# One GpSimd subtraction of 1024 columns in place of four of 256, in a float32 block whose weights are split in two

## The reference

```python
u = rmsnorm(x, norm_mix) * (1 + scale1) + shift1        # scale, shift, gate from cond @ ada_w
aq, ak, av, bq, bkv, biq, bik, biw, cq, ck, cv, g = split_cols(u @ w_in)
y_a, y_b, y_c = diff_attention(...), dsa_attention(...), moba_attention(...)   # each @ its own w_br
x = x + gate1 * ((gates[0]*y_a + gates[1]*y_b + gates[2]*y_c) @ w_o)
x = x + gate2 * (square(relu(u2 @ w_ff1)) @ w_ff2)
for layer in range(2):                                  # the second block
    proj = rms_norm(x, pre_norm[layer]) @ w_in_2[layer]
    y_conv = c_b * causal_depthwise_conv(c_c * c_x) * silu(c_z)
    y_ret = retention_chunkwise(rotary(q), rotary(k), v), normalised, * silu(r_z)
    x = x + rms_norm(concat(y_conv, y_ret) @ w_out[layer], post_norm[layer])
```

## Time and profile before

| | us |
|---|---|
| median of three runs | 1036.79 |
| the three runs | 1036.6, 1036.79, 1037.68 |
| the profiled execution, its own time | 1037.68 |
| its span in the profile | 1035.6 |
| busy: PE, DVE, ACT, POOL | 971.7, 597.0, 489.9, 737.7 |

### The profile page before, as it was taken

One profiled execution on the slowest core, in us unless ns is written; L12 is line 12 of the kernel. 1 busy time (PEld: TensorE's weight loads), 2 busy tenths in 40 slices (PEclk: granted clock), 3 DMA queues, 4 the chain that ended last, 5 costly groups with the idle time before them and its releaser, 6 DMA issues.

```text
span 1035.6 us, 21952 instructions
## 1 busy us (share of the span) xinstructions
PE 971.7 (94%) x7796; PEld 946.8 (91%) x7796; DVE 597.0 (58%) x978; ACT 489.9 (47%) x803; POOL 737.7 (71%) x916
## 2 busy tenths in 40 slices
PE   0599999999899999999999999999999999999997
PEld 0598889899789999999999999999999999999996
DVE  5748896664888555111465557765245555676612
ACT  2344656554345555444344446444444444644441
POOL 6666746666785888777466667999746666699973
PEclk9999999999999999999899999999999999999999
DMA  8956445555553546645244444554523444454521
GB/s 324 382 199 244 164 163 203 204 187 185 198 204 122 204 162 216 240 174 181 103 164 163 151 146 153 205 197 164 180 107 122 163 162 155 138 196 166 199 103 41
DMA packets 28079, 184.68 MB, mean 178 GB/s; under 512 B 3011, under 2 KB 5488, under 8 KB 6128
## 3 DMA queue, kind: packets, MB, share of 16 engines
q1 hardware_dynamic: 25832, 167.54, 45.0%
q10 hardware_dynamic: 2184, 16.27, 4.3%
HBM read 182.73 MB, written 1.07 MB: 177 GB/s over the span
## 4 chain that ended last, share of the span: by engine, by line
PE 83%; DVE 10%; ACT 3%; issue 2%; POOL 1%; DMA 1%; SPq 0%; POOLq 0%; DVEq 0%; ACTq 0%
PE mm L518 24%; PE mm L520 24%; PE mm L519 23%; DVE ada_acc L1342 3%; PE mm L551 1%; PE mm L539 1%; PE mm L540 1%; PE mm L541 1%; PE ps_t L578 1%; DVE w_lo L1320 1%; DMA ada_raw<-ada 1%; ACT w_hi L941 1%; PE ps_s L839 1%; PE ps_o L854 1%; PE ps_o L890 1%
## 5 line engine op out<-in xcount | busy, mean ns | idle before, releaser
L423 POOL TENSOR_TENSOR w_lo<-raw,w_hi 128x256 fp32r<-128x256 f32 x872 | 699.1, 836 | 244.2 <-ACT w_hi L941 243.5
L518 PE MATMUL mm<-u_hi,w_hi 128*128 128x256 f32 x1608 | 466.3, 290 | 1.9 <-issue 1.9
L520 PE MATMUL mm<-u_hi,w_lo 128*128 128x256 f32 x1608 | 454.8, 283 | 0.0
L519 PE MATMUL mm<-u_lo,w_hi 128*128 128x256 f32 x1608 | 454.8, 283 | 0.0
L941 ACT ACTIVATE w_hi<-raw 128x1024 fp32r<-128x1024 f32 x291 | 306.8, 1055 | 167.2 <-PE mm L520 167.2
L518 PEld LDWEIGHTS mm<-u_hi,w_hi 128*128 128x128 f32 x1608 | 308.1, 192 | 8.0 <-issue 7.5
L519 PEld LDWEIGHTS mm<-u_lo,w_hi 128*128 128x128 f32 x1608 | 308.2, 192 | 2.1 <-issue 1.9
L520 PEld LDWEIGHTS mm<-u_hi,w_lo 128*128 128x128 f32 x1608 | 307.9, 191 | 0.0
L1320 DVE TENSOR_TENSOR w_lo<-raw,w_hi 128x1024 fp32r<-128x1024 f32 x72 | 94.1, 1307 | 122.6 <-ACT w_hi L941 120.8
L518 PE MATMUL mm<-mix_hi,w_hi 128*128 128x256 f32 x256 | 71.9, 281 | 0.2
L520 PE MATMUL mm<-h_hi,w_lo 128*128 128x256 f32 x256 | 71.9, 281 | 0.0
(11 more groups left out here) (280 smaller groups left out, 1305.7 us busy)
## 6 DMA issues: line engine op xcount, KB each, us to landing
raw<-weights SPq DMA_DIRECT2D x145, 1024.0 KB, 4.8
ada_raw<-ada ACTq DMA_DIRECT2D x14, 1024.0 KB, 4.9
ada_raw<-ada SPq DMA_DIRECT2D x6, 1024.0 KB, 8.0
ada_more<-ada SPq DMA_DIRECT2D x4, 1024.0 KB, 9.2
bias<-tab_scratch SPq DMA_DIRECT2D x1, 1536.0 KB, 10.6
dec<-decay ACTq DMA_DIRECT2D x1, 1536.0 KB, 7.1
x<-xT SPq DMA_DIRECT2D x1, 1024.0 KB, 15.3
out<-x SPq DMA_DIRECT2D x4, 256.0 KB, 2.2
```

Of the source, the lines that this page charges most:

```text
L423: ins = nc.gpsimd.tensor_tensor(w_lo[:, s, at], r[:, at], hi[:, at], ALU.subtract)
L518: nc.tensor.matmul(dst, wh, rhs_hi(k), start=a, stop=False)
L519: nc.tensor.matmul(dst, wh, rhs_lo(k), start=False, stop=False)
L520: i = nc.tensor.matmul(dst, wl, rhs_hi(k), start=False, stop=b)
```

## The change

In POOL's `low`, the four subtractions over a quarter of the unit each (256 columns) become one over all 1024 columns. The semaphore `lo_pool` was raised by the last of the four and is now raised by the one instruction, by the same amounts. Nothing else changes: the same units, the same waits ahead of them, the same slots.

```diff
             r = raw[:, (c // 2) % RAW_PAIRS, (c % 2) * KC * P:(c % 2 + 1) * KC * P]
             s = c % SLOTS
-            hi = w_hi[:, s, :].bitcast(F32)
-            quarter = KC * P // 4
-            for e in range(4):
-                at = slice(e * quarter, (e + 1) * quarter)
-                ins = nc.gpsimd.tensor_tensor(w_lo[:, s, at], r[:, at], hi[:, at], ALU.subtract)
-            ins.then_inc(S["lo_pool"], 3 if c == 2 else 2 if c % 4 == 2 else 1)
+            nc.gpsimd.tensor_tensor(w_lo[:, s, :], r, w_hi[:, s, :].bitcast(F32), ALU.subtract)\
+                .then_inc(S["lo_pool"], 3 if c == 2 else 2 if c % 4 == 2 else 1)
```

## The result

The changed kernel takes 1107.95 us in the median of four runs (1103.44 to 1108.39), the one before 1037.24 in the same comparison (1036.6 to 1039.5, four runs). The ratio is 1.065, with a 95% interval of 1.062 to 1.068: slower by 71 us. The prediction had the direction, and a size of 24.6 us. It is wrong by a factor of almost three. In all, 39 executions of the changed kernel are on record, in two groups: 21 between 1100.3 and 1104.3 us and 18 between 1106.6 and 1110.8. By its span the profiled one belongs to the lower group.

A forecast was written before the change was run, and what follows sets the result against it. The prediction took PE as the bound (busy 94%, 83% of the chain), with DVE on 10% of the chain. Gains of 3.3 and losses summed to +24.6 on 1036.8 us: 1061.4, say 1061, range 1041 to 1080.

The forecast's parts named there:

- Price of the long operation: POOL's subtraction over 1024 columns: 2.33 us, against 2.90 for four pieces; bounds 2.0 and 2.9.
- Rival 1: The lock is let go within the long instruction, so only gains stay: 1032 us; chance 0.07.
- (a) to (c): Start-up and one later unit: PE gets w_lo sooner, gains of 1.3, 1.6 and 0.4, together -3.3 us.
- (d): Retention heads: POOL holds kr, PE waits; six turns at 1.36 and two at 0.8 make +9.8 us.
- kr(0): The earlier kr in a retention turn: no longer slips in between two pieces, POOL is first, +0.33 us.
- kr(1): The later kr in a retention turn: held by POOL, +0.5 us alone; both kr's late together, 1.36 a turn.
- (e): End of the convolution heads, twice: three POOL units delay DVE's tail, PE waits 3.4 each, +6.8 us; the loop costs nothing.
- (f): Branch outputs, 258 to 284: six POOL units each cost DVE 1.73, 10.4 less 5.1 lost today: +5.3 us.
- (g): Output projection and norm, 288.75 to 313: six units at 1.7, less 4.2 lost today and 3 idle: +3.0 us.
- (h): Attention, 103 to 139: five contacts at 1.7, less 4 today, a third covered by waits for ScalarE: +3 us.
- Feed-forward and out-projections: FFN (323 to 498) and two later output projections: PE sets the pace, 0, bounds -0.5 to +2 us each.
- Rival 3: DVE's lags pile up in four convolution and feed-forward loops, 2 to 5 us each: 1078 us; chance 0.12.

The follow-up runs named there:

- E3: The changed kernel with four pieces again for the units of the retention heads (135 to 166, 215 to 246): 1089.39 us, ratio 1.049.
- E7: The changed kernel with ScalarE's copy mix_hi of the retention output one unit later in its order: 1101.28 us, ratio 1.061.
- E12: The kernel before, with one long instruction for units 55 to 70 (branch outputs, output projection and norm): 1049.16 us, ratio 1.011.
- E11: The kernel before, with one long instruction for units 25 to 54 (attention from 139 us on): 1048.34 us, ratio 1.012.
- E9: POOL does every unit in eight pieces of 128 columns, against four in the kernel before: 1084.88 us, ratio 1.047.
- E6: The kernel before, with one long instruction for the last eight units of each convolution stage: 1052.49 us, ratio 1.017.

## Why the prediction was right in kind and wrong in size

- **Price of the long operation:** 2.33 predicted, 2.34 at least and 2.41 in the median. Right.
- **The lock holds for a whole instruction at 1024 columns:** right, by kr at 573.89. Rival 1 is out. DVE's growth of 131 us was put at 30 to 90.
- **(a) to (c), start-up and w_lo:** -2.9 and -0.4 predicted, -3.6 and -0.8 (unit 74) measured. Right.
- **(d) Retention heads:** +9.8 predicted, 1.36 a turn; +11.8 measured, 1.45 a turn, and E3 returns 12.3. Right in size, with both kr's late in each turn. Its two parts were split otherwise: kr(0) costs 0.69 and not 0.33 (the rows of the prediction make that 0.29), kr(1) another 0.76 and not 1.03.
- **(e) Convolution heads: this is the step that failed.** It said that DVE "lags by some 2 us per turn of four units and holds there", and costed the loop at nothing, on the cover of PE's four banks. DVE's lag doesn't hold. Three blocked operations of 5.7 us in all make its turn 12.98 us long, against PE's 11.52, so the lag grows from turn to turn. Nor is it the banks that PE meets first, but w_lo, POOL's behind ScalarE's late w_hi and DVE's own; only with ScalarE's copy moved (E7) is it the banks. The loops cost 4.9 and 5.2. The end was put at 3.4 with DVE arriving on time; it arrives late, and PE's wait of 6.8 is followed by 6 us at half clock, a cost for which the prediction had no term. 6.8 predicted, 28 measured. The prediction named the price of being wrong, "2 us more for each layer" without cover, but as a cost per layer and not as one that piles up.
- **(f) Branch outputs:** +5.3 predicted, +6.7 measured (E12: +6.3). Right in size. It isn't m_lo, as I had said, but the sum of two SBUF tiles, merged, that is hit six times in eight units at 2.05 to 2.52 us; m_lo is now at 418 ns throughout (the earlier trace rows had 942).
- **(g) Output projection and norm:** +3.0 predicted, +7.8 measured (E12: +6.8). The mechanism is the one named; too small by the average of 1.7 per contact less "4.2 lost today", where three contacts in a row end on PE's wait for acc, and by the clock of 0.80.
- **(h) Attention:** +3 predicted for 103 to 139, and +3.1 measured for units 7 to 18, all of it at unit 16 (115 us before the change). But the stage goes on to 246. From 139 on I had no term at all, because the chain that I read ended there, and units 19 to 50 lose 12.1 (E11: 10.8). PE waits there for DVE's prob (4.0 us, 0 before), for ScalarE's o_var (4.3, before 1.1) and a little longer for two others; which contacts make these late was not taken apart.
- **Feed-forward and out-projections:** 0 predicted. No loss (-1.8 with its norms).

By size the missing 40 us (64.4 - 24.6) are: 21 in (e), 12 in the part of attention without a term, 5 in (g), 3.4 in (d) and (f), less 2.1 of greater gains where w_lo comes sooner and at the norms. Rival 3, lags that pile up, comes nearest. It had 0.12 and, at 1078, was itself too low. Of its four loops the two of the convolution heads lose 4.9 and 5.2, the top of its 2 to 5, by the in-order queue of ScalarE that it named; the feed-forward loops lose nothing. The 12 us in attention were in no rival.

The changed kernel's median, 1107.95, is of its upper group, some 6 us above the profiled execution; no trace shows where those are.

## What to carry to other kernels

In this kernel a VectorE operation with its inputs in SBUF that met a reading GpSimd instruction of 256 to 1024 columns waited for its end (kr: 0.27 and 0.28 us after it), so the length of a GpSimd instruction is a price that VectorE pays at each contact. Shorter isn't always better: at 128 columns VectorE was passed over. Before joining or splitting one, ask in each stage how long VectorE may be held before somebody waits, and whether it has idle time to catch up; where it has none, the price adds up from turn to turn. Cost every stage, those too that the chain of before only brushes. And add to any new wait of TensorE of several us what it then loses at the lower clock.

## What the runs showed of the hardware

- Operations of DVE with an operand in PSUM were never held, in any trace and at any length of POOL's. First such an operation in the changed kernel, 32 times, then one without, 16 times (ns least, median, most):

```profile
L1694 DVE TENSOR_TENSOR rt<-mm,cosT x32: 411/420/425, 543.0 to 927.4; 128x256 f32<-128x256 f32 x32
```

```profile
L1786 DVE TENSOR_SCALAR cy<-cv,vec x16: 355/1916/2061, 658.8 to 1033.6; 128x256 f32<-128x256 f32 x16
```

- The second row has one SBUF tile as its input and is held all the same, in 14 of 16 executions; before the change it was in 4. The counts in (f) to (h) of the prediction went by operations with two SBUF inputs and left such ones out. The Trainium skill, "SBUF — State Buffer", section "Who interferes with whom", has `tensor_scalar` among the operations that can enter a mode with two ports and then contend; the trace agrees, with 1916 ns against 355.
- Very short pieces don't share better: of 128 columns, 31 in a row shut DVE out for 14 us (E9).
- In waits of 5.1 (E6) and 6.8 us (changed kernel) TensorE's granted clock fell to 0.50, and it stayed there for another 4.1 and 6.0 us of work; the half of these was lost on top of the wait.
